# Seven block products in place of eight in the first feed-forward product of a decoder layer

## The reference, cut to what matters

```python
h = rms_norm(x, ln2_pre_l) * (1 + sc2) + sh2
f = jnp.square(jax.nn.relu(h @ w_ff1_l)) @ w_ff2_l
x = x + g2 * rms_norm(f, ln2_post_l)
```

## Time and profile before

| | us |
|---|---|
| median of 3 runs | 855.14 |
| lowest, highest | 855.03, 862.37 |
| profiled execution, whole | 857.43 |
| its span, first to last instruction | 855.8 |
| TensorE busy in the span | 809.6 |
| VectorE, ScalarE, GpSimd busy | 434.2, 325.8, 111.5 |

### The profile page before, as it was taken

One profiled execution on the slowest core, in us unless ns is written; L12 is line 12 of the kernel. 1 busy time (PEld: TensorE's weight loads), 2 busy tenths in 40 slices (PEclk: granted clock), 3 DMA queues, 4 the chain that ended last, 5 costly groups with the idle time before them and its releaser, 6 DMA issues.

```text
span 855.8 us, 12676 instructions
## 1 busy us (share of the span) xinstructions
PE 809.6 (95%) x4882; PEld 652.1 (76%) x4882; DVE 434.2 (51%) x812; ACT 325.8 (38%) x628; POOL 111.5 (13%) x157
## 2 busy tenths in 40 slices
PE   6899999999989989799979999999999999999987
PEld 2577557788745566477769988999889988899875
DVE  0533758999669964324746322244334334334355
ACT  4544533233356744323664322333203422234231
POOL 2044303259424420010000000000000000000000
PEclk9999999998999999699999999999999999999999
DMA  8924310313278799553013232221231222231203
GB/s 318 350 75 126 108 50 17 94 50 118 90 268 278 248 302 368 185 193 114 0 50 100 99 99 64 84 99 50 98 98 52 98 99 75 73 100 56 93 0 111
DMA packets 68783, 105.92 MB, mean 124 GB/s; under 512 B 6986, under 2 KB 32214, under 8 KB 68714
## 3 DMA queue, kind: packets, MB, share of 16 engines
q1 hardware_dynamic: 64194, 96.48, 34.0%
q0 software_dynamic: 3296, 6.39, 2.5%
q10 hardware_dynamic: 1232, 2.23, 0.7%
HBM read 100.04 MB, written 5.15 MB: 123 GB/s over the span
## 4 chain that ended last, share of the span: by engine, by line
PE 87%; DVE 4%; DMA 3%; ACT 3%; issue 2%; SPq 1%; POOL 0%; DVEq 0%; ACTq 0%
PE bank L793 83%; PE bank L796 4%; DMA pages<-in_cache_k 1%; DMA raw<-in_w_in 1%; SPq L597 1%; ACT w_split L1414 1%; ACT stage L1439 1%; DMA raw<-in_ada_w 1%; DVE probs L2077 0%; DMA cst<-in_consts 0%; DVE keys L1849 0%; DVE probs L2089 0%; DVE act_lo L1849 0%; DVE w_split L517 0%; POOL near L735 0%
## 5 line engine op out<-in xcount | busy, mean ns | idle before, releaser
L793 PE MATMUL bank<-tok_hi,w_split 128*128 128x288 f32 x1024 | 206.0, 295 | 4.2 <-DVE tok_lo L1849 3.6
L793 PEld LDWEIGHTS bank<-tok_hi,w_split 128*128 128x128 f32 x1024 | 164.5, 188 | 5.5 <-ACT tok_hi L1439 2.7
L517 DVE TENSOR_TENSOR w_split<-raw,w_split 128x2048 fp32r<-128x2048 f32 (+2 forms) x45 | 101.7, 2259 | 114.5 <-ACT w_split L1414 114.4
L793 PE MATMUL bank<-w_split,hid_hi 128*128 128x512 f32 x512 | 158.9, 392 | 0.0
L793 PE MATMUL bank<-tok_lo,w_split 128*128 128x288 f32 x512 | 150.8, 294 | 0.0
L1414 ACT ACTIVATE w_split<-raw 128x2048 fp32r<-128x2048 f32 (+2 forms) x48 | 89.4, 1863 | 91.8 <-PE bank L793 89.5
L793 PEld LDWEIGHTS bank<-w_split,hid_hi 128*128 128x128 f32 x512 | 96.0, 188 | 20.7
L793 PE MATMUL bank<-act_hi,w_split 128*128 128x512 f32 (+1 forms) x288 | 100.3, 406 | 1.9 <-DVE act_lo L1849 1.8
L793 PE MATMUL bank<-w_split,hid_lo 128*128 128x512 f32 x256 | 100.1, 391 | 0.0
L793 PEld LDWEIGHTS bank<-tok_lo,w_split 128*128 128x128 f32 x512 | 96.0, 188 | 0.1
L1439 ACT ACTIVATE stage<-bank 128x288 f32<-128x288 f32 (+3 forms) x83 | 36.9, 447 | 112.0 <-PE bank L793 108.5
(11 more groups left out here) (261 smaller groups left out, 1110.3 us busy)
## 6 DMA issues: line engine op xcount, KB each, us to landing
raw<-in_w_ff SPq DMA_DIRECT2D x32, 1024.0 KB, 5.4
raw<-in_ada_w SPq DMA_DIRECT2D x18, 1024.0 KB, 5.1
raw<-in_w_in SPq DMA_DIRECT2D x10, 1024.0 KB, 5.5
pages<-in_ada_w SPq DMA_DIRECT2D x6, 1024.0 KB, 8.2
pages<-in_cache_k SPq DMA_DIRECT2D x24, 256.0 KB, 4.8
v_pages<-in_cache_v SPq DMA_DIRECT2D x24, 256.0 KB, 5.9
raw<-in_w_out SPq DMA_DIRECT2D x4, 1024.0 KB, 7.9
x_in<-in_x_prompt SPq DMA_DIRECT2D x1, 2048.0 KB, 10.5
```

The lines of the kernel that those rows point to most:

```text
L517: return ops.tensor_tensor(lo, r, hi.bitcast(F32), ALU.subtract)
L793: return nc.tensor.matmul(out, lhsT, rhs, start=start, stop=stop, skip_group_check=True)
```

## The change

For p = 1 to 15 the pair's product is cut in blocks: token halves x = 0, 1, width halves k = 0, 1 (4 chunks each), column blocks j = 0, 1. Instead of eight block products there are seven (`PRODUCTS`), each of 12 matmuls of 288 columns. With A(k,x) the tokens and W(k,j) the weights:

- P1 = A(0,0) W(0,0); C11 goes on in P1's bank with A(1,0) W(1,0);
- P6 and P67 share a bank, with mixed tokens `mix2` and `mix3`; P5 (`mix1`) and P53 (A(1,1)) share one; P4 (with `tok[0:4, x=1]`, overwritten by a mix) has its own;
- the weights of P5, P6, P67 and P53 are sums and differences of the W(k,j), made by GpSimd, four operations of 512 columns a pair, in `w_sums`.

P1, P6 and P5 are read out between the two products that share their bank: ScalarE copies P1 out (`p1_kept`), VectorE makes `u2_kept` = P6 + P1 and `u3_kept` = P67 + P1, and the other outputs by three more sums. The ReLU moves into VectorE's square (`max(x, 0) * x`). Each pair uses four banks, 0 to 3 and 4 to 7 in turn. The token mixes are made once, during pair 0, by GpSimd (three differences of 1152 columns), VectorE, and splits by all three.

Weights from pair 1 on are split in units of 512 columns, high and low together 4 KB a row: seven per pair, four per w2 piece, in eight rooms, each taken again when the product that read it is done. The untransposed x goes to DRAM (`x_saved`, five stores on ScalarE's queue) and comes back by GpSimd's queue after pair 15, so that its room can hold the mixes. The normalised tokens stand in `x_nrm2`. `gates(1)` moves between the token chunks.

```diff
@@ plan_banks, after them PRODUCTS and plan_rooms
-            for u in range(4):
-                take(("w1", 8 * f + 2 * i + u // 2, u % 2), (4 * i + u) % 3)
+            p = 4 * f + i
...
+            a, b, c, d = (0, 1, 3, 2) if p % 2 == 0 else (4, 5, 7, 6)
+            take(("P1", p), a), take(("P6", p), b), take(("C11", p), a), take(("P67", p), b)
+            take(("P5", p), c), take(("P4", p), d), take(("P53", p), c)
...
+PRODUCTS = ("P1", "P6", "C11", "P67", "P5", "P4", "P53")
@@ gpsimd
+            pool.wait_ge(S["h_hi"], KC + 4)
+            pool.wait_ge(S["h_low"], KC + 4)
+            difference(part(0, 1), part(0, 1), part(0, 0))
+
+            def weight_sums(p):
...
+                pool.wait_ge(raw_landed[raw_slot(n)], landed_at[n])
+                s1, s2, s3, s4 = (w_sums[:, j] for j in range(4))
+                if p > 1:
+                    pool.wait_ge(S["unit_lo"], UNIT_NO["P5", p - 1])
+                nc.gpsimd.tensor_tensor(s1, quarter(p, 0, 1), quarter(p, 1, 1), ALU.add).then_inc(S["summed"], 1)
+                pool.wait_ge(S["summed"], 4 * (p - 1) + 1)
+                nc.gpsimd.tensor_tensor(s2, s1, quarter(p, 0, 0), ALU.subtract).then_inc(S["summed"], 1)
+                nc.gpsimd.tensor_tensor(s3, quarter(p, 0, 0), quarter(p, 0, 1), ALU.subtract).then_inc(S["summed"], 1)
...
+                nc.gpsimd.tensor_tensor(s4, quarter(p, 1, 0), s2, ALU.subtract).then_inc(S["summed"], 1)
...
+            weight_sums(1)
+            pool.wait_ge(S["mix2_raw"], 4)
+            difference(part(0, 0), part(1, 1), part(0, 0))
+            difference(part(1, 0), part(1, 0), part(1, 1))
...
+            for p in range(2, 4 * QF):
+                weight_sums(p)
@@ tensor
+            def product_steps(product, p):
...
+                pe.wait_ge(S["unit_lo"], UNIT_NO[product, p])
+                out = claim((product, p))
+                more = product in ("C11", "P67", "P53")
+                for k in range(4):
+                    mm(out[:, 0:HN], hi[:, k, :], x_hi[:, k, :], k == 0 and not more, False)
+                    mm(out[:, 0:HN], hi[:, k, :], x_lo[:, k, :], False, False)
+                    last = mm(out[:, 0:HN], lo[:, k, :], x_hi[:, k, :], False, k == 3)
@@ scalar
+            def pair_outputs(p, more):
+
+                if more:
+                    hi_units(1)
+                if p > 1 and p % 4:
+                    hidden_hi(2 * p - 2, 2 * p)
...
+                free(run(p1_kept[:, :], full(act, ("P1", p))[:, 0:HN]), ("P1", p))
+                if more:
+                    hi_units(2)
...
+                free(run(stage_tok[:, 0, 0, :], full(act, ("C11", p))[:, 0:HN]), ("C11", p))
+                if more:
+                    hi_units(4)
+                hidden_hi(2 * p + 1, 2 * p + 1)
@@ vector
+            def pair_outputs(p, more):
+
+                if more:
+                    lo_units(1)
+                if p > 1 and p % 4:
+                    hidden_lo(2 * p - 2, 2 * p)
+                evacuated(dve, ("P1", p))
+                add(u2_kept[:, :], "P6", p, p1_kept[:, :])
+                if more:
+                    lo_units(2)
+                add(u3_kept[:, :], "P67", p, p1_kept[:, :])
...
+                add(stage_tok[:, 1, 1, :], "P5", p, u3_kept[:, :])
...
+                add(stage_tok[:, 1, 0, :], "P4", p, u3_kept[:, :])
+                squared_relu(p, 2 * p + 1)
...
+                add(stage_tok[:, 0, 1, :], "P53", p, u2_kept[:, :])
+                squared_relu(p, 2 * p)
+                hidden_lo(2 * p + 1, 2 * p + 1)
```

More of the change, by code:

```diff
@@ L1096, in by_token @@
                 for half in range(2):
-                    hi, lo, _ = piece(kind, first + half)
+                    if kind == "w2":
+                        parts = [unit_parts(("w2", first + half, c)) for c in range(4)]
+                        hi, lo = [x[0] for x in parts], [x[1] for x in parts]
+                    else:
+                        both = piece(kind, first + half)
+                        hi, lo = [both[0][:, c, :] for c in range(4)], [both[1][:, c, :] for c in range(4)]
                     if f is not None:
@@ L1479, in turned_hidden @@
                     n = k * KC + kc
-                    if k * KC + kc >= 2:
+                    if k == 0 and kc >= 2:
                         act.wait_ge(S["h_low"], n - 1)
-                    free(run(stage[:, kc % 2, :], out[:, :], ACT.Identity,
+                    made = h_raw[:, kc, :, 0:HP] if k else stage[:, kc % 2, :]
+                    free(run(made, out[:, :].rearrange("p (x n) -> p x n", x=2) if k else out[:, :], ACT.Identity,
                              scale=mod_t[:, 16 * k + 8 + kc, 0:1], bias=mod_t[:, 16 * k + kc, 0:1]), ("hT", k, kc))
```

354 lines of the change are left out of this document (285 added, 69 removed).

## The result

| | us |
|---|---|
| median of 4 runs (lowest, highest) | 886.88 (881.14, 890.74) |
| the kernel before, 4 runs beside it | 855.09 (850.12, 862.37) |
| ratio, 95% interval | 1.036 (1.032 to 1.040) |
| profiled execution; its span | 890.74; 888.9 |

The account below looks back on a forecast made before the run. TensorE, busy 95% of the span, was taken as the bound. Profiled 857.43 + 11.4 (head) - 1.0 (pairs 2 and 3) + 0.9 (three later groups) = 868.7, less 2.29: 866 us, range 840 to 880.

Parts of the forecast that it names:

- the period of a pair: From one P6 sum to the next: the larger of TensorE's 11.15 us and VectorE's round.
- the clock: TensorE's lower clock level: nothing in the sum, priced only in Rival (4).
- Matmuls, floor, VectorE's own work: Feed-forward pairs: 180 matmuls fewer save 23.9 us, floor 831.2 us; VectorE needs 9.9 of 11.15 us a pair.
- The steady pairs: Three later groups: VectorE rounds of 13.65 and 13.25 us make each first product 51.3 us against 51.0, +0.3 each.
- The price of a sum: Pairs with GpSimd weight sums: each 512-column sum shuts VectorE out of SBUF for 0.9 us.
- The head: Pairs 0 and 1: TensorE waits before the fourth unit and C11, pair 1 ends at 475.1, +11.4; without port waits +5.9.
- Rival (4): Head: idle stretches of 4 and 7 us may lower TensorE's clock, +4, 870 us; chance within the forecast's 0.42.
- pairs 2 and 3: Rest of the first group: 13.3 + 11.15 us against 25.5, -1.0; with the port shared gently -3.2.
- (3): SBUF port held for GpSimd's whole operation: rounds of 15.9 and 14.8, groups +4.8 each, head +14.5; 885 us, chance 0.12.
- (1): SBUF port shared gently: VectorE's 9.9 stays under 11.15, head +5.9, later groups -5.7 each; 841 us, chance 0.25.
- (2): GpSimd gets the port only when VectorE pauses: 0.4 a sum, groups -3.5 each, head +9.5; 852 us, chance 0.20.
- (5): The change does not do what it says, against TensorE's list of seven products a pair; at most 1 in 100.

Follow-up runs that it names:

- e1_no_port: Changed kernel with the weight sums of pairs 2 to 15 replaced by GpSimd constant writes, results not kept; 852.0 us, ratio 0.998.
- e24_both: Changed kernel with the edits of e2_sums_on_vector and e4_handover_order together; 873.9 us, ratio 1.023.
- e2_sums_on_vector: Changed kernel with the weight sums of pairs 2 to 15 made by VectorE instead of GpSimd; 885.1 us, ratio 1.034.
- e4_handover_order: Changed kernel with the previous pair's even-output hand-over moved behind the copy of P1 and the sum of P6 in pairs 2 to 15; 888.2 us, ratio 1.040.
- e8_no_head_port: e1_no_port with pair 1's weight sums and GpSimd's token mixes also replaced by constant writes; single run, 847.6 us.

## Why the prediction was wrong

Right were the direction (the forecast gave "slower" a chance of 0.45) and the places. Who waits for whom was right in the head and half right in the groups; the size was not right: profiled against profiled, 890.7 against the sum's 868.7. The missing 22.0 us are 13.1 in the first stage (80.5 against 57.0 + 11.4 - 1.0 = 67.4), less 2.5 as it began earlier, and 11.3 in the groups (+12.2 against +0.9). **Two steps failed: the period of a pair, taken as the larger of two engines' rounds, where the engines wait for each other in turn; and the clock, which the sum had at nothing.**

**Matmuls, floor, VectorE's own work: right.** 1356 matmuls of 288 columns; a free group takes 44.9 us (4 x 11.15 = 44.6 was the reckoning), VectorE needs 9.3 us a pair where 9.9 was forecast.

**The steady pairs.** The sums of P6 in the third group end at T+7.2, 23.0 and 38.0, and the group at 55.7; forecast T+6.8, 20.4, 33.7 and 51.3. The rounds are 15.8 and 15.0 against 13.65 and 13.25 (in the second group 17.3 and 14.3, in the fourth 14.7 and 15.0). These two rounds, and then one of e1_no_port:

```profile
674.60:690.43 15.83, 13.60 (x83) 13.42 (x84) 14.67 (x18) 6.59 (x14) 9.31 (x6) 0.83 0.37 123
690.43:705.40 14.97, 12.43 (x87) 11.99 (x86) 12.93 (x18) 6.53 (x14) 6.79 (x4) 0.95 0.22 70
```

```profile
566.57:577.70 11.13, 11.13 (x87) 11.13 (x86) 9.49 (x19) 6.29 (x13) 1.99 (x4) 1.00 0.28 98
```

The price of a sum came out: four cost VectorE 12.93 - 9.49 = 3.4 us, 0.86 each, where 0.9 was taken, though the parts are others (1.10 for a split, 0.6 for a square, nothing for a bank sum). So VectorE's own round is 12.9 us, less than the 13.25 forecast; for the other 2.0 us it stood idle. It waited for products of TensorE, which had itself waited 2.1 us for the copy of P1 and then ran at the lower clock. Neither engine's round sets the period: TensorE is idle for 2.5 us of this one and VectorE for 2.0. The sum had VectorE at work without a pause.

**The clock.** On TensorE's side 9.0 of the 11.3 us missing in the groups are busy time: e1_no_port's TensorE is busy for 44.8 us in a group, this one's for 47.3, 48.8 and 47.2 with the same matmuls, while its idle time, 7.3, 7.0 and 7.3 us, is close to the 51.3 - 44.6 = 6.7 forecast. 6.7 of the 9.0 lie in the four stretches at granted clock 0.50; the rest, under 1 us a group, also stands in groups with waits at clock 1.00 (e24_both's 45.9). The waits that the forecast itself reckoned with had to be priced at the low clock in the range, too.

**That VectorE's round alone sets the period: half right.** ScalarE was said to fit with 6.6 us of 11.15, which is true of its amount; but its copy of P1 stands behind a hand-over from VectorE. e2_sums_on_vector and e4_handover_order show that the two limits are nearly of a size.

**The head.** The order of events was right: TensorE idle before the fourth unit, then before C11 until the copy at 468.7 (forecast 467.0). But pair 1 ended at 483.7 and not at 475.1. C11 to the end of pair 1 took 14.4 us in place of 8.1: TensorE ran at the lower clock from 466.7 to 480.3, busy for 8.8 us there, and waited 2.2 us for the sum of P6. All in all 12.7 of the first stage's 28.3 us are TensorE busy longer. Rival (4) had named this, for two stretches only, at 4 us. The token differences of 1152 columns held a split for 3.11 - 0.69 = 2.4 us, where 1.9 was taken. Without GpSimd's reads e8_no_head_port has +8.9 for the head (forecast +5.9, which keeps GpSimd's own time) and -3.2 for pairs 2 and 3, as forecast. In the changed kernel these two pairs took 26.5 us where 25.4 stood before: +1.1, not -1.0.

**The rivals.** (3) comes nearest in the number, 885, and in its rounds, 15.9 and 14.8, but by luck: a hold for all of GpSimd's operation is not what happens, it is 1.10 of 1.28 us, and the waits in turn and the low clock stood where it had put the port. The Trainium skill (SBUF — State Buffer, "Who interferes with whom") calls the shared pair of ports an exclusive lock, and has it held "for the whole instruction" in its sentence on VectorE's two-port modes; here, with two inputs in SBUF, the two engines do shut each other out, but the hold is 0.55 us for 256 columns and 1.10 for 512, shorter than the recorded operation. (1) and (2) fall: splits beside GpSimd took 1.79 us, and both engines took turns at nearly every operation (at 563.75 GpSimd was kept out by three). (5) falls by the count.

## What to carry to other kernels

When a removed matmul leaves more for the engines beside it, the question is not only whether their work fits into the shorter period, but in which order each takes what TensorE waits for. Two engines that wait for each other in turn have a longer period than either one's work, and two such limits of the same size hide each other: an edit that lifts one shows little. Each wait put on TensorE's path is to be priced with a stretch at the lower clock behind it as the upper bound, by the difference of busy time for the same matmuls. Preparatory work for a cheaper algorithm belongs under the stretch that still runs the old one: three more pairs left with eight products cost 4.8 us of matmuls and made the first stage 12.0 us shorter all the same.
